# Decoder block on eight cores: the gate norm's root on GpSimd, mixing in two banks of its own, and a second pair of output weight tiles loaded ahead

## What is computed

```
h    = rmsnorm(x, g_mix)
proj = h @ w_in                                  # u | v | z, 1024 columns each
u, v = gelu(proj[..., :1024]), gelu(proj[..., 1024:2048]);  z = proj[..., 2048:]
vh   = rmsnorm of v over each head of 128 columns, times g_v        # the gate norm
out_a = u * (tril(W_s) vh + b_s)                 # chunks of 128 tokens, 8 heads: the mixing
out_b = (trailing mean of z over 2/4/8/16 - z) @ w_pool * pool_scale
x = x + concat(out_a, out_b) @ w_out
x = x + relu(rmsnorm(x, g_ffn) @ w_up)^2 @ w_down        # 8192 hidden columns
return rmsnorm(x, g_final)
```

## Time and profile before

| | |
|---|---|
| runs of the kernel before | 1257.12, 1275.77, 1485.61 us (median 1275.77) |
| profiled execution | 1256.82 us, span 1255.3 us on the slowest core |
| spans of the 8 cores | 1252.3 to 1255.3 us |
| granted TensorE clock, mean | 0.989 to 0.991 of 2.4 GHz |
| busy: PE, PEld, DVE, ACT, POOL | 96%, 44%, 27%, 20%, 5% |
| v stage and its mixing | about 147 to 217 us |
| output projection | about 217 to 342 us |

### The profile page before, as it was taken

How to read it: one execution, slowest core, us unless ns; L and a number is a source line. 1 busy time by engine, 2 the same in 40 slices (tenths; PEclk the granted TensorE clock), 3 DMA queues, 4 the chain that set the end, 5 groups by cost and what they waited for, 6 DMA issues and landing times.

```text
span 1255.3 us, 14349 instructions; the slowest of 8 cores (1252.3 to 1255.3 us)
## 1 busy us (share of the span) xinstructions
PE 1206.0 (96%) x5736; PEld 547.6 (44%) x5736; DVE 335.0 (27%) x550; ACT 252.0 (20%) x473; POOL 66.3 (5%) x97
## 2 busy tenths in 40 slices
PE   5899999899999999999999999999999999999994
PEld 2354444344444444444444444444444444444441
DVE  3565556312112121211112121212121121211234
ACT  2401287223321110001111000111100011123332
POOL 0100000000000000000000000000000000000000
PEclk9999999899999999999999999999999999999997
DMA  8995510987656445545554554455455545559985
GB/s 272 228 176 83 83 37 2 158 165 147 133 79 83 74 67 85 82 68 73 83 80 67 79 85 72 68 84 85 68 72 86 78 68 77 87 83 141 144 170 172
DMA packets 37921, 126.95 MB, mean 101 GB/s; under 512 B 2784, under 2 KB 2912, under 8 KB 36832
## 3 DMA queue, kind: packets, MB, share of 16 engines
q0 software_dynamic: 24912, 95.43, 51.9%
q1 hardware_dynamic: 12944, 30.61, 7.9%
HBM read 213.05 MB, written 8.39 MB: 176 GB/s over the span
## 4 chain that ended last, share of the span: by engine, by line
PE 92%; ACT 2%; DMA 2%; DVE 2%; issue 1%; SPq 1%; DVEq 0%; ACTq 0%
PE ps L217 81%; PE ps L652 8%; DMA xf<-xT 2%; PE ps L404 1%; PE ps L842 1%; SPq L235 0%; ACT L589 0%; PE ps L316 0%; ACT sqv L599 0%; DVE xr_h L808 0%; DVE xr_mid L808 0%; PE ps L682 0%; PE ps L681 0%; PE ps L355 0%; ACT pooled L569 0%
## 5 line engine op out<-in xcount | busy, mean ns | idle before, releaser
L217 PE MATMUL ps<-h2T,ringall 128*128 128x512 bf16 x2048 | 442.8, 379 | 0.0
L217 PEld LDWEIGHTS ps<-h2T,ringall 128*128 128x128 bf16 x2048 | 200.4, 98 | 241.6
L217 PE MATMUL ps<-pooled,ringall 128*128 128x512 bf16 x1024 | 234.1, 379 | 0.0
L217 PE MATMUL ps<-uT,ringall 128*128 128x512 bf16 x1024 | 234.1, 379 | 0.0
L767 DVE SCALAR_TENSOR_TENSOR rtmp<-ps,rstd_bc 128x512 f32<-128x512 f32 x128 | 82.5, 686 | 360.9 <-PE ps L217 351.2
L217 PEld LDWEIGHTS ps<-pooled,ringall 128*128 128x128 bf16 x1024 | 100.2, 98 | 120.8
L217 PEld LDWEIGHTS ps<-uT,ringall 128*128 128x128 bf16 x1024 | 100.2, 98 | 120.8 <-issue 0.3
L772 ACT ACTIVATE uT<-rtmp 128x512 bf16<-128x512 f32 x64 | 39.1, 629 | 505.9 <-DVE rtmp L767 505.9
L217 PE MATMUL ps<-hT,ringall 128*128 128x512 bf16 x384 | 83.7, 379 | 0.0
L772 ACT ACTIVATE pooled<-rtmp 128x512 bf16<-128x512 f32 x64 | 39.3, 629 | 181.7 <-DVE rtmp L767 181.7
L652 PE MATMUL ps<-uT,ringall 128*128 128x512 bf16 x256 | 60.1, 390 | 4.4 <-DVE uT L545 4.4
(11 more groups left out here) (98 smaller groups left out, 527.8 us busy)
## 6 DMA issues: line engine op xcount, KB each, us to landing
ringall<-w_down POOLq DMA_DIRECT2D x40, 1024.0 KB, 10.5
ringall<-w_up POOLq DMA_DIRECT2D x32, 1024.0 KB, 10.5
ringall<-w_in POOLq DMA_DIRECT2D x10, 1024.0 KB, 12.0
xf<-xT SPq DMA_DIRECT2D x8, 1024.0 KB, 20.9
ringall<-w_out POOLq DMA_DIRECT2D x8, 1024.0 KB, 15.8
xstage<-xT SPq DMA_DIRECT2D x16, 512.0 KB, 13.3
wstg<-w_in SPq DMA_DIRECT2D x4, 1024.0 KB, 16.1
outT<-xr_h SPq DMA_DIRECT2D x16, 256.0 KB, 4.0
```

Of the source, the lines that this page charges most:

```text
L217: ins = e.matmul(ps[:, banks[sel], c0:c1], lhsT, rhs, start=st, stop=sp_)
```

## The change

Three parts:

- The root of the gate norm is made on GpSimd: `vstat / 128 + EPS` (a TENSOR_SCALAR on 128 x 8 numbers) and then that to the power of -0.5 (a TENSOR_TENSOR with the constant `mhalf`), in place of Ln and Exp on ScalarE.
- `emit_mixing` always uses banks 6 and 7 and takes none from the ring.
- Output weight tiles 2 and 3 have a buffer of their own, `wx`, loaded on GpSimd's queue behind slab 12, once pooling is done. The ring's slabs of the output projection are then seven (13 holds tiles 4 and 5, and so on), and `head_pool(2)` stands behind mixing 7 and ahead of the second gate halves.

```diff
+    wx = sb("wx", [128, 2, KC, 128], BF16, X0 + 16384 + 6 * 4096)
-    for j in range(8):
+    for j in (0, 2, 3, 4, 5, 6, 7):
         slabs.append(w_out_d[:, 2 * j:2 * j + 2, :, :])
+    mhalf_op = P.add("dve", lambda e: e.memset(mhalf[:, :], -0.5))
     issue_loads(12)
+    wx_ld = P.dma("pool", lambda e: e.dma_start(out=wx[:, :, :, :], in_=w_out_d[:, 2:4, :, :]), "wx", [pool_all])
-            ba = take_bank() if own_banks is None else own_banks[hb]
+            ba = 6 + hb
-        q3 = P.add("act", lambda e, s=s: e.activation(out=vrs[:, s, :], in_=vstat[:, s, :], func=AF.Ln, bias=EPSB, scale=1.0 / 128), [q2, eps_op])
-        q4 = P.add("act", lambda e, s=s: e.activation(out=vrs[:, s, :], in_=vrs[:, s, :], func=AF.Exp, scale=-0.5), [q3])
+        q3 = P.add("pool", lambda e, s=s: e.tensor_scalar(out=vrs[:, s, :], in0=vstat[:, s, :], scalar1=1.0 / 128, scalar2=EPS, op0=ALU.mult, op1=ALU.add),
+                   [q2, vst_readers[s]])
+        q4 = P.add("pool", lambda e, s=s: e.tensor_tensor(out=vrs[:, s, :], in0=vrs[:, s, :], in1=mhalf[:, :], op=ALU.pow), [q3, mhalf_op])
+    issue_loads(12 + NSLOT - 1)
     head_pool(0)
-    emit_mixing(6, [6, 7])
+    emit_mixing(6)
     head_pool(1)
     head_gate(0, 0)
     head_gate(1, 0)
-    emit_mixing(7, [6, 7])
-    head_gate(0, 1)
-    head_gate(1, 1)
-    issue_loads(12 + 1 + NSLOT - 1)
+    emit_mixing(7)
     head_pool(2)
-    head_gate(2, 0)
-    head_gate(2, 1)
+    for m, half in ((0, 1), (1, 1), (2, 0), (2, 1)):
+        head_gate(m, half)
```

More of the change, by code:

```diff
@@ L170, in build_program @@
     vstat = calloc("vstat", [128, 2, 8], F32, 64)
+    mhalf = calloc("mhalf", [128, 8], F32, 32)
     vrs = calloc("vrs", [128, 2, 8], F32, 64)
@@ L527, in build_program, with emit_mixing @@
     mt_ctr = [0]
-    def emit_mixing(i, own_banks=None):
+    def emit_mixing(i):
         for hb in range(2):
-            ba = take_bank() if own_banks is None else own_banks[hb]
+            ba = 6 + hb
             def fn(e, ba=ba, hb=hb):
@@ L643, in flush_one, with wo_slab, wo_w @@
                 rexp2[half] = P.add("act", lambda e, c0=c0, c1=c1: e.activation(out=rstd_bc[:, c0:c1], in_=rstd_bc[:, c0:c1], func=AF.Exp, scale=-0.5), [ln])
+    def wo_slab(m):
+        return None if m // 2 == 1 else 12 + max(m // 2 - 1, 0)
+    def wo_w(m, k):
+        n = wo_slab(m)
+        return wx[:, m % 2, k, :] if n is None else RS(n, k, (m % 2) * 128, (m % 2 + 1) * 128)
     def wo_part(m, banks, ks, halves, deps):
-        n = 12 + m // 2
+        n = wo_slab(m)
         def fn(e):
@@ L651, in fn @@
                 for half in halves:
-                    ins = e.matmul(ps[:, banks[half], :], RS(n, k, (m % 2) * 128, (m % 2 + 1) * 128), MIX(k)[:, half * 512:(half + 1) * 512],
+                    ins = e.matmul(ps[:, banks[half], :], wo_w(m, k), MIX(k)[:, half * 512:(half + 1) * 512],
                                    start=(k == K_POOL[0]), stop=(k == K_GATE[-1]))
             return ins
-        return P.add("pe", fn, [slab_ld[n]] + deps)
+        return P.add("pe", fn, [wx_ld if n is None else slab_ld[n]] + deps)
     def wo_evac(m, half, job, bank):
@@ L700, in head_pool @@
     def head_pool(m):
-        issue_loads(12 + m // 2 + NSLOT - 1)
         wo_part(m, hb[m], K_POOL, [0, 1], ob_deps + [bank_last[b] for b in hb[m]])
@@ L705, in head_gate @@
         job = wo_part(m, hb[m], K_GATE, [half], [mix_tile_last[3 if half == 0 else 7]])
-        slab_done[12 + m // 2] = job
+        if m < 2:
+            slab_done[wo_slab(m)] = job
         wo_finish(m, job, half, hb[m][half])
+    issue_loads(12 + NSLOT - 1)
     head_pool(0)
-    emit_mixing(6, [6, 7])
+    emit_mixing(6)
     head_pool(1)
@@ L726, in build_program @@
         job = wo_part(m, banks, K_POOL + K_GATE, [0, 1], [bank_last[b] for b in banks])
-        slab_done[n] = job
+        if n is not None:
+            slab_done[n] = job
         wo_last = job
@@ L737, in build_program @@
     x2_e1 = list(x1_e[0])
-    nbase = 20
+    nbase = 19
     r2 = [None]
```

## The result

The changed kernel takes 1245.38 us, median of 4 runs (1244.24 to 1247.18), and the ratio to the kernel before is 0.991, with a 95% interval of 0.9886 to 0.9935: faster by 0.9%, clear of zero, and within the 2% that is called the same. The forecast was 1244.4 in 1241 to 1260. Of the four runs of the kernel before that go with it (1256.48, 1257.12, 1275.77 and 1485.61 us) the last two are disturbed executions, and the ratios and medians from here on leave such runs out. In the comparisons of the study the kernel before then has medians of 1256.2 to 1257.2.

A forecast was written before the change was run, and what follows sets the result against it. TensorE was taken as the bound (92% of the chain), with time to win only where it idles or runs at the lower clock: 1256.8 - 6.2 (v stage) - 7.2 (tail) + 1.0 (output stage) = 1244.4 us, range 1241 to 1260.

The forecast's parts named there:

- the tail: From the mixing behind v tile 7 to output tile 3: 7.2 us less, from 4.4 idle, 2.3 clock, 0.5 short gaps.
- v stage, -6.2: From v tile 3 to the mixing behind v tile 7: 6.2 us of TensorE idle in four gaps would go.
- P: Tail: time from where the second table load stood (end of ScalarE's squares) to vh of tile 7; taken as 1.0 us.
- limit of 1.83: Tail: TensorE waits for nothing ahead of the second gate halves as long as P is under 1.83 us.
- pair slower than 1.83: Rival: GpSimd's root pair exceeds 1.83 us, each further microsecond costing one in the tail; P = 6 gives 1248.6; chance 0.13.
- Clock, 2.3: Tail: 16 matmuls at half clock behind the 4.41 us wait lost 2.27 us, which would be won back.
- Output stage, +1.0: Output tiles: TensorE waits for tile squares whose residual is loaded late; 1.4 less a margin of 0.4 us.
- 4.5 later ... hidden, by 13: Four slab loads behind the last root issue 4.5 us later; first needed by tile 4, so hidden with 13 us spare.
- one for one, whatever waits behind: Slab and xstage queues share packets equally (379 and 385 in 12 us), regardless of backlog, so the sum stays.
- xstage queues behind the slabs: Rival: tile 2's residual waits for the fourth slab, 255.8; TensorE waits 7.1 us, clock falls (2.3); 1252.8 us; chance 0.12.
- Table load returned: Ln ahead of the up projection needs a load again, +1.28 us on its first evacuation, hidden.
- The pair that sets the period: Rival: GpSimd's pair so slow it lengthens each v tile above 9.1 us; break-even P near 10; chance 0.04.

The follow-up runs named there:

- undo_root: The changed kernel with the root back on ScalarE as Ln and Exp; measured 1247.46 us, ratio 0.9925 to the kernel before.
- undo_banks: The changed kernel with mixing 0 to 5 taking its banks from the ring again; measured 1249.98 us, ratio 0.9939 to the kernel before.
- pow2: The changed kernel with one more power on GpSimd ahead of each root, into scratch; measured 1247.51 us, ratio 0.9921 to the kernel before.
- undo_wx: The changed kernel without the early pair wx, jobs ahead of tile 3 in the old order; measured 1249.93 us, ratio 0.9942 to the kernel before.
- loads_first: The changed kernel with the four slab loads ahead of the last root on GpSimd's queue; measured 1242.80 us, ratio 0.9896 to the kernel before.
- pow5: The changed kernel with four more powers on GpSimd ahead of each root, into scratch; measured 1256.90 us, ratio 1.0001 to the kernel before.

## Why the prediction came out right

The time and its sign were right, the forecast 1.0 below the median and 1.9 below the profiled execution (1244.4 against 1246.34). These 1.9 are 0.4 of the tail, 0.1 of the output stage, 0.24 at the start of v tile 3 and 1.1 of stores. Two of the signs of being wrong showed, both small: TensorE waited 0.23 for VectorE's product ahead of the second gate halves and 0.96 for sqr in the output stage.

**v stage, -6.2: right.** -6.18, on all cores. That both parts are needed, each for half, was not in my text; undo_root and undo_banks show it.

**P: mis-sized.** I took 1.0 us between bounds of 0.2 and 1.6. Groups of the page on GpSimd, after (count | busy, mean ns | idle before):

```profile
L607 POOL TENSOR_TENSOR vrs<-vrs,mhalf 128x8 f32<-128x8 f32 x8 | 13.1, 1640 | 1.5 <-POOL vrs L605 0.5
...
L605 POOL TENSOR_SCALAR vrs<-vstat 128x8 f32<-128x8 f32 x8 | 2.5, 318 | 50.5 <-ACT sqv L603 50.5
```

And the last root in the timelines of ScalarE, GpSimd and VectorE, core 7:

```profile
215.41 0.19 ACT L603 ACTIVATION_READ_ACCUMULATOR sqv<-vf 128x1 f32 x1
215.81 0.20 POOL L605 TENSOR_SCALAR vrs<-vstat 128x8 f32<-128x8 f32 x1 [5.39 <-ACT sqv L603]
216.16 1.64 POOL L607 TENSOR_TENSOR vrs<-vrs,mhalf 128x8 f32<-128x8 f32 x1
217.74 2.94 POOL L284 DMA_DIRECT2D ringall<-w_out  x4
217.90 2.19 DVE L612 SCALAR_TENSOR_TENSOR vh<-vf,vrs,gv_t 128x128 bf16<-128x128 f32 x8 [2.38 <-POOL vrs L607]
```

The squares end at 215.60 (215.41 + 0.19) and vh starts at 217.90: P is 2.3, above both bounds. The failed step is the upper one, two DMA issues of 0.72: a row of another kind is no bound for an operation that was never timed. The limit of 1.83 held: 0.47 beyond it gave 0.4 in TensorE's start (226.62 by the sum, 227.02 measured) and in the tail (-6.77 for -7.2). The rival "pair slower than 1.83" (chance 0.13) is therefore what happened, at its mildest end, and one power more (pow2) costs the 1.60 that this rival's rule says.

The largest of the eight powers took 1667 ns and the smallest 1635, so the first call is not told from the rest. The Trainium skill (GPSIMD Engine Reference, Instruction dispatch) has 5.95 us for the first call of freshly loaded code; this case's rows do not show it for the power.

**Clock, 2.3: right.** Window of after over the tail, with the granted clock at 1.00:

```profile
227.00:235.00 8.00, 7.98 (x37) 3.64 (x38) 1.38 (x2) 4.08 (x4) 0.72 (x1) 1.00 1.00 159
```

undo_wx qualifies it: with 3.7 us of idle the clock fell on six cores, among them core 4, and stayed on core 3 and core 7. In before, all 8 cores paid it (tail 29.41 to 29.96).

**Output stage, +1.0: the size right, the cause wrong.** +1.12 on the slowest core is close to the forecast by luck. I had it build up over the even pairs, 1.4 from tile 2 to tile 8, less a margin of 0.4 that is 0.56 by the numbers it was taken from (253.56 and 254.12), so that the sum would have been +0.8. It came at once on the slowest core, at the odd tile 3, and loads_first, which leaves the evacuations' period as it is, has next to none of it. The step that failed is the one on the slabs: "4.5 later ... hidden, by 13" (5.6 later, measured, since P was 2.3) prices a late load only for who waits for its data, and "one for one, whatever waits behind" takes the residual's transfer time as given. One for one is right (88 and 88 packets), as the Trainium skill has it too (DMA: Bandwidth & Descriptors, Queues, rings and completion order: the engines go round the queues packet by packet). But one for one holds only as long as q0 has packets, so how long the backlog lasts decides when q1 gets three times its pace. The rival "xstage queues behind the slabs" (tile 2 evacuated only at 255.8, 9.4 us lost) did not occur in that form: tile 2 took 14.3 us, like before's 14.8.

**Table load returned: right.** The first evacuation of the up projection, in the timeline of VectorE of after, core 7:

```profile
343.00 1.29 DVE L778 SCALAR_TENSOR_TENSOR rtmp<-ps,rstd_bc 128x512 f32<-128x512 f32 x2 [10.94 <-ACT rstd_bc L648]
```

It is 10.30 earlier than in rows 11, where the up projection starts 11.59 earlier: 1.29 late, as forecast, and hidden.

**The pair that sets the period: the break-even too high, and its way wrong.** I put it near P = 10, by a period above 9.1. pow5 has P near 8.9 (after's 2.3 and four powers more, 6.6) and is at 1.0001 of before, where my rule would have left 5.3 us of the gain (12.4 less 7.1). The rule took 9.1 for the period of every v tile, while tiles without a pooling job are 6.9 to 7.4 apart, so that a root of 8.6 already falls behind; and it left out VectorE's queue, which passes the delay of a root on to the products that free the next mixing's banks.

Open stays why the output stretch of one kernel differs among cores (by 2.6 us in after, 4.1 in undo_banks) though they run the same program, and whether the 1.1 of the stores belongs to the change: each compares one core of one execution with another, and starts of v tile 3 alone differ from 164.5 to 168.2 among after's cores.

## What to carry to other kernels

An operation whose price has no row gets a range that starts at the nearest rows and goes past them, and the sum says up to which price it is free; here that limit (1.83) was worth more than the estimate (1.0). A load that is issued later costs not only who waits for its data: it moves the stretch in which its queue takes every other packet, and each small transfer that another queue has in that stretch takes longer. And an engine's wait for a late input stands in front of all that is queued behind it, so work that is ready goes ahead of it.

## What the runs showed of the hardware

- A power of 128 x 8 float32 numbers on GpSimd takes 1.64 us (1635 to 1667 ns), another one behind it 1.60 (pow2) to 1.72 (pow5, 6.88 for four). The multiply and add on the same numbers took 0.19 to 0.20 where VectorE was idle for most of it, and 0.40 to 0.46 where VectorE was busy beside it, four times each on cores 0, 3, 4 and 7 of after (the mean of core 7's eight is 0.32).
- The hardware queue moved 88 packets in 3 us beside a software queue with work and 297 in 3 us in which that ran empty; beside the backlog a transfer of 512 KB came 14 to 22 us after its buffer was free.
- Of two cores that idled 3.68 and 3.69 us in one execution at the same place, one was granted 0.50 of 2.4 GHz behind it and the other 1.00 (undo_wx, cores 4 and 3).
